# Beside the expert matrix of a two-layer block: five early blocks ahead of the picks, and a main part that begins with a parked unit

## The chip, the cores and the metric

One core of a Trainium2 chip runs the whole computation in one launch. The metric is the device time in microseconds, the median of several runs. Beside the runs there is one profiled execution, whose trace is read below. Its engines are named PE (TensorE, matmuls), PEld (TensorE's weight loads), DVE (VectorE), ACT (ScalarE), POOL (GpSimd) and SP (SyncE, which only issues transfers here).

## What is computed

256 tokens of width 1024 pass through a first transformer block and then a second one. What matters here is the last layer of the second, a product-key mixture of experts with 16384 experts, in float32:

```python
def peer(h, w_q, sub_keys, u, v):            # h: 256 tokens x 1024
    ...
        q = (xb @ w_q).reshape(tb, PEER_HEADS, 2, PEER_DKEY // 2)
        s = jnp.einsum('thpd,hpnd->thpn', q, sub_keys).astype(jnp.float32)
        sv, si = lax.top_k(s, k)                       # 16 best of 128, per head and half
        ...
        top_v, top_i = lax.top_k(cand, k)              # 16 best pairs per head
        experts = jnp.take_along_axis(cand_idx, top_i, axis=-1)
        g = jax.nn.softmax(top_v, axis=-1)
        u_e = u[experts]
        v_e = v[experts]
        a = jax.nn.gelu(jnp.einsum('td,thkd->thk', xb, u_e).astype(jnp.float32), approximate=False)
        return jnp.einsum('thk,thkd->td', (g * a).astype(xb.dtype), v_e)
```

After it come the gated residual and a final norm.

## The kernel before

The kernel gathers no rows. It computes GELU(u · h) for all 16384 experts, multiplies it with a matrix G that holds the weight of each expert for each token (zero for nearly all), and multiplies the result with all of v. The experts are cut into 64 units of 256. A unit of u is 1 MB in two blocks of 1024 words a partition; so does a unit of v.

Each block of weights comes by a transfer into one of 5 ring slots. ScalarE rounds it to a high part (line 1051), and VectorE (line 1437) or GpSimd (line 2085) makes the low part by subtraction; `lo_on_pool` says which. TensorE multiplies high with high, high with low and low with high. Every engine has its own program and runs it in order; `hi_until`, `lo_until` and `load_until` do their part for all blocks up to a key and `AHEAD` = 3 more (1 more in the part beside G on ScalarE and VectorE).

The last layer has three stretches.

1. **Selection** (`SELECT_ORDER`). The scores and the top-16 searches run on VectorE, with help of GpSimd. TensorE meanwhile makes the query panels and the first 11 units of u (`feature_panel`, lines 654 and 659: a block is 16 matmuls with the high part of u and 8 with the low part). The GELU of an early unit is stored to HBM ("parked", `early_out`, line 1345).
2. **The expert matrix** (`expert_matrix_order`). The picks, that is rows, columns and weights of the chosen experts, are transposed (line 1008) once VectorE has made the weight (line 1972). Then come 64 steps of G: VectorE and ScalarE build matrices of zeros and ones (lines 1984, 1388, 1987, 1994), TensorE multiplies them (line 1017), ScalarE copies the one half of a bank to G (line 1375), VectorE adds the other (line 2001). Between the steps stand the blocks of 36 more early units, numbers 11 to 46. Block b belongs to unit 11 + b // 2; 11b stands for the second block of unit 11, and so on. The picks come behind two blocks; three blocks stand between picks and the first step of G. ScalarE takes an early unit's GELU four entries of the order later.
3. **The main part** (`UNIT_ORDER`). It goes through all 64 units. The 17 late ones (47 to 63) are made there by `unit_panel` (lines 681 and 686), summed on VectorE (lines 2035, 2036), GELU on ScalarE (line 1404). The 47 parked ones are loaded from HBM to one of three hid buffers. These buffers lie where G's selection matrices lay. Either kind is multiplied by G on VectorE (line 2042), rounded on ScalarE (line 1406), and its left part is made on VectorE (line 1738, which gives `hid_lo`). Then `rows_onto` (lines 716 and 721) multiplies it with the rows of v, two places in the order later (`V_LAG` = 2), onto four banks `peer_acc`. The order before begins 47, 0, 1, 48, 2, 3, 4, 49.

TensorE takes banks with `take`, which gives the longest idle of the eight and waits until its last user has emptied it. In the second stretch three banks serve u (`u_banks`), four serve picks and G (`G_banks`), and one holds constants ("numbers"). At its end the idle ones stand in this order: those of units 44 and 45, the two of G's step 62, the two of step 63, that of unit 46, and the constants'. Before the first panel of the main part, the program takes four for `peer_acc`, then two for unit 47.

SyncE's program loads the parked unit of place `at + 1` behind the blocks of place `at`; each load waits until its buffer is free.

## Time and profile before

| | |
|---|---|
| runs | median 1392.35 us (1391.27 to 1392.82, 3 runs) |
| profiled execution | 1391.79 us |
| its span, first to last instruction | 1390.0 us |
| mean granted clock of TensorE | 0.992 |
| PE busy | 1351.1 us (97%) |
| DVE busy | 1017.1 us (73%) |
| ACT busy | 756.5 us (54%) |
| POOL busy | 460.1 us (33%) |
| HBM read / written | 270.34 MB / 14.94 MB |

Times in the trace are microseconds from the start of the span. In this execution the picks are transposed at about 692 us, G's steps go from 702 to 923 us, and the main part follows. A line of the timeline gives start and duration, engine, source line, what is written and read, and in brackets the idle time of that engine just before and what ended it. Consecutive matmuls are pipelined, so the duration of one line overlaps the next by some tenths; the difference of two starts is the exact pace.

### The profile page before, as it was taken

To read this page: it belongs to the slowest core of one execution; us is meant where nothing else is said; L and a number is where in the kernel's file an instruction comes from. 1 tells how busy PE (TensorE), PEld (TensorE's weight loads), DVE (VectorE), ACT (ScalarE), POOL (GpSimd) and SP (SyncE) were. 2 spreads that over 40 slices of the span, in tenths; PEclk is the share of its full clock that TensorE was granted. 3 is DMA by queue.
4 is the path that set the end of the run, shared out by engine and by line. 5 is a ranking of instruction groups with operands and counts; after the bars stand their busy time and mean duration, and the time that the engine had idled before them with its cause. 6 is when DMAs were issued, how large, how long until landed. Compare 5 with 4: busy or idle time off the path is not lost.

```text
span 1390.0 us, 21698 instructions
## 1 busy us (share of the span) xinstructions
PE 1351.1 (97%) x8475; PEld 1214.4 (87%) x8475; DVE 1017.1 (73%) x1834; ACT 756.5 (54%) x1201; POOL 460.1 (33%) x264
## 2 busy tenths in 40 slices
PE   9999999999999999999799999989999999999997
PEld 7898889999988777999799999987888888888885
DVE  5676686888867675799888888865666666667666
ACT  5555745444656454554477777754444544544543
POOL 2630000000034102798867777641222222222221
PEclk9999999999999999999999999999999999999999
DMA  7553247879878624467566666654757756767665
GB/s 250 179 146 103 78 172 244 277 266 326 274 245 284 242 99 167 137 207 226 175 185 199 200 191 195 207 184 166 232 200 227 235 197 232 234 198 229 231 200 211
DMA packets 194645, 286.69 MB, mean 206 GB/s; under 512 B 9664, under 2 KB 121024, under 8 KB 194288
## 3 DMA queue, kind: packets, MB, share of 16 engines
q1 hardware_dynamic: 186800, 270.12, 60.2%
q10 hardware_dynamic: 7344, 13.95, 2.6%
q0 software_dynamic: 400, 1.25, 0.4%
q8 instruction: 67, 1.10, 0.3%
q14 instruction: 34, 0.28, 0.1%
HBM read 270.34 MB, written 14.94 MB: 205 GB/s over the span
## 4 chain that ended last, share of the span: by engine, by line
PE 81%; DVE 11%; ACT 2%; DMA 2%; POOL 1%; issue 1%; DVEq 0%; ACTq 0%
PE bank L716 19%; PE bank L654 19%; PE bank L721 10%; PE bank L659 9%; PE bank L627 6%; PE bank L681 5%; PE bank L631 3%; PE bank L686 2%; PE bank L1017 2%; DMA sb_raw<-w_in 1%; PE bank L931 1%; PE bank L950 1%; DVE sb_in_row L1930 1%; PE bank L809 1%; DVE sb_eq L1936 1%
## 5 line engine op out<-in xcount | busy, mean ns | idle before, releaser
L2085 POOL TENSOR_TENSOR sb_lo<-sb_raw,sb_hi 128x1024 fp32r<-128x1024 f32 (+1 forms) x162 | 387.7, 2402 | 596.4 <-ACT sb_hi L1051 596.4
L1051 ACT ACTIVATE sb_hi<-sb_raw 128x1024 fp32r<-128x1024 f32 (+2 forms) x428 | 442.3, 1046 | 202.5 <-DMA sb_raw<-w_in 43.0
L1437 DVE TENSOR_TENSOR sb_lo<-sb_raw,sb_hi 128x1024 fp32r<-128x1024 f32 (+2 forms) x266 | 357.0, 1357 | 159.8 <-ACT sb_hi L1051 158.5
L654 PE MATMUL bank<-sb_act,sb_hi 128*128 128x256 f32 x2720 | 357.4, 284 | 0.7 <-DVE sb_act L1523 0.7
L654 PEld LDWEIGHTS bank<-sb_act,sb_hi 128*128 128x128 f32 x2720 | 340.3, 192 | 2.3 <-issue 1.3
L716 PE MATMUL bank<-sb_hi,sb_hid_hi 128*128 128x512 f32 x600 | 234.8, 391 | 4.1 <-DVE sb_hid_lo L1738 4.1
L716 PE MATMUL bank<-sb_hi,sb_hid_lo 128*128 128x512 f32 x600 | 234.5, 391 | 0.0
L659 PE MATMUL bank<-sb_act,sb_lo 128*128 128x256 f32 x1360 | 191.2, 283 | 2.3 <-POOL sb_lo L2085 2.3
L659 PEld LDWEIGHTS bank<-sb_act,sb_lo 128*128 128x128 f32 x1360 | 175.3, 192 | 3.1 <-POOL sb_lo L2085 3.1
L721 PE MATMUL bank<-sb_lo,sb_hid_hi 128*128 128x512 f32 x600 | 161.0, 389 | 0.0
L716 PEld LDWEIGHTS bank<-sb_hi,sb_hid_hi 128*128 128x128 f32 x600 | 113.3, 189 | 27.1 <-DVE sb_hid_lo L1738 4.3
L716 PEld LDWEIGHTS bank<-sb_hi,sb_hid_lo 128*128 128x128 f32 x600 | 113.3, 189 | 22.9
L721 PEld LDWEIGHTS bank<-sb_lo,sb_hid_hi 128*128 128x128 f32 x600 | 112.6, 188 | 23.4
L1406 ACT ACTIVATE sb_hid_hi<-sb_hid 128x512 fp32r<-128x512 f32 x64 | 40.5, 632 | 127.5 <-DVE sb_hid L2042 127.5
L2091 POOL TENSOR_TENSOR sb_stat<-sb_stat 128x1 f32<-128x1 f32 (+1 forms) x19 | 12.6, 673 | 281.8 <-DVE sb_stat L1467 234.1
L1984 DVE TENSOR_TENSOR sb_hot<-bank,sb_pick_T 128x1024 fp32r<-128x1024 f32 x64 | 78.4, 1224 | 31.8 <-PE bank L1017 31.8
L1738 DVE TENSOR_TENSOR sb_hid_lo<-sb_hid,sb_hid_hi 128x512 fp32r<-128x512 f32 x75 | 51.9, 693 | 52.4 <-ACT sb_hid_hi L1406 44.7
L627 PE MATMUL bank<-sb_hi,sb_act 128*128 128x512 f32 (+1 forms) x352 | 83.9, 380 | 1.0 <-DVE sb_act L1523 0.6
L1453 DVE CUSTOM_DVE_ANT_0 sb_ada_junk<-sb_ada_w,sb_c_rows 128x1024 bf16<-128x1024 f32 x64 | 79.4, 1275 | 0.0
L627 PEld LDWEIGHTS bank<-sb_hi,sb_act 128*128 128x128 f32 x352 | 63.2, 188 | 13.1 <-ACT sb_hi L1051 1.9
L681 PE MATMUL bank<-sb_act,sb_hi 128*128 128x512 f32 x272 | 68.6, 395 | 3.2 <-DVE sb_G L2001 3.2
L681 PEld LDWEIGHTS bank<-sb_act,sb_hi 128*128 128x128 f32 x272 | 50.4, 190 | 13.2 <-issue 3.4
(346 smaller groups left out, 1581.5 us busy)
## 6 DMA issues: line engine op xcount, KB each, us to landing
sb_raw<-peer_uT SPq DMA_DIRECT2D x128, 512.0 KB, 4.0
sb_raw<-peer_v SPq DMA_DIRECT2D x128, 512.0 KB, 4.5
sb_raw<-w_in SPq DMA_DIRECT2D x52, 512.0 KB, 4.5
sb_ada_w<-ada_wT SPq DMA_DIRECT2D x48, 512.0 KB, 6.0
parked_units<-sb_early ACTq DMA_DIRECT2D x47, 256.0 KB, 4.1
sb_hid<-parked_units SPq DMA_DIRECT2D x47, 256.0 KB, 2.7
sb_raw<-w_gate SPq DMA_DIRECT2D x22, 512.0 KB, 4.0
sb_raw<-w_up SPq DMA_DIRECT2D x22, 512.0 KB, 5.1
```

The source lines that it names most:

```text
L627: e.matmul(opened[t][:, 0:n], part[:, k0 + k, t * P:(t + 1) * P], hi[:, k, :], start=i == first_i and k == 0 and part is x.hi, stop=False)
L654: e.matmul(bank[:, j * T:(j + 1) * T], hi[:, k, j * P:(j + 1) * P], part[:, k0 + k, :], start=i == first_i and j == 0 and k == 0 and part ...
L659: ins = e.matmul(bank[:, j * T:(j + 1) * T], lo[:, k, j * P:(j + 1) * P], x.hi[:, k0 + k, :], start=False, stop=i == last_i and j == 1 and ...
L681: e.matmul(bank[j][:, :].rearrange("p (w t) -> p w t", w=2), hi[:, k, j * P:(j + 1) * P], act_both[:, k0 + k], start=first and k == 0, sto ...
L716: e.matmul(psum(acc, 2 * half_ + t)[:, :], part[:, k, t * P:(t + 1) * P], hi[:, k, :], start=first and k == 0 and part is hid.hi, stop=False)
L721: ins = e.matmul(psum(acc, 2 * half_ + t)[:, :], hid.hi[:, k, t * P:(t + 1) * P], lo[:, k, :], start=False, stop=last and k == 1)
L1051: e.activation(flat_of(i, "hi"), flat_of(i, "raw"), ACT.Copy).then_inc(hi_done[i % R], 1)
L1437: e.tensor_tensor(flat_of(i, "lo"), flat_of(i, "raw"), flat_of(i, "hi").bitcast(F32), ALU.subtract).then_inc(lo_done[i % R], 1)
L1453: e.tensor_tensor_reduce(ada_junk[n % 2], ada_bufs[b], c_rows[:, row], 1.0, 0.0, ALU.mult, ALU.add, mcol[name][:, c:c + 1]).then_inc(*ada_ ...
L1738: e.tensor_tensor(hid_pair[i].lo, hid_raw[i], hid_pair[i].hi.bitcast(F32), ALU.subtract).then_inc(*hid_lo.inc(*unit))
L1984: e.tensor_tensor(h[:, :, 0:3:2, :].rearrange("p t w n -> p w t n"), iota_p.unsqueeze(1).unsqueeze(1).to_broadcast([P, 2, TG, P]), pT[:, 0 ...
L2085: e.tensor_tensor(flat_of(i, "lo"), flat_of(i, "raw"), flat_of(i, "hi").bitcast(F32), ALU.subtract).then_inc(lo_done[i % R], 1)
```

## The change

- `expert_matrix_order`: the picks come behind five blocks of u, and the first step of G behind nine (`b + 1 - G_FROM` is first positive at b = 8), so four blocks stand between them. 38 early units stand there instead of 36, so 49 units are parked and 15 are late.
- `UNIT_ORDER`: the main part begins with parked unit 0, and goes on 49, 1, 2, 3, 50, 4, 5, 6, 51. Three times four parked units stand in a row, where before there were at most three.
- TensorE takes the banks of `peer_acc` only with v's first rows, behind the first late unit's panel.
- ScalarE and VectorE make the high and low parts of the first late unit's blocks between G's last two sums.
- SyncE loads the first parked unit ahead of the main loop, once G's step 62 is full.

```diff
-EARLY_BESIDE_G = 36
+EARLY_BESIDE_G = 38
...
-G_FROM = 4
+PICKS_FROM, G_FROM = 5, 8
...
-UNIT_ORDER = [v for k in range(N_LATE) for v in (EARLY + k, *range(k * EARLY // N_LATE, (k + 1) * EARLY // N_LATE))]
+UNIT_ORDER = [0] + [v for k in range(N_LATE) for v in (EARLY + k, *range(1 + k * (EARLY - 1) // N_LATE, 1 + (k + 1) * (EARLY - 1) // N_LATE))]
...
-        if b == G_FROM // 2 - 1:
+        if b == PICKS_FROM - 1:
             yield "picks", 0, 0
...
-            for b in range(4):
-                take("peer_acc", b)
             for at in range(N_UNITS + V_LAG):
                 if at < N_UNITS and UNIT_ORDER[at] >= EARLY:
                     whole(unit_panel(UNIT_ORDER[at], h2))
                 if at >= V_LAG:
                     v = at - V_LAG
+                    if v == 0:
+                        for b in range(4):
+                            take("peer_acc", b)
                     rows_onto("peer_acc", ("v", v), ("peer", v), v == 0, v == N_UNITS - 1)
...
-            for q in range(N_G - HOT_BUFS, N_G):
-                G_rounded(q)
+            G_rounded(N_G - 2)
+            hi_until(("uT", UNIT_ORDER[1]), None, 0)
+            G_rounded(N_G - 1)
...
-            for q in range(N_G - HOT_BUFS, N_G):
-                G_sum(q)
+            G_sum(N_G - 2)
+            lo_until(("uT", UNIT_ORDER[1]), None, 0)
+            G_sum(N_G - 1)
...
+            def load_hid(at):
+                i, u = at % HID_BUFS, UNIT_ORDER[at]
+
+                sp.wait_ge(*(hid_used["peer", at - HID_BUFS] if at >= HID_BUFS else full("G", N_G - (1 if at else 2), TG - TG_BANK)))
+                b, nth = early_slot(u)
+                sp.wait_ge(early_stored[b], 16 * (nth + 1))
+                e.dma_start(hid_raw[i], parked_units[u].rearrange("p (c t) -> p c t", t=T)).then_inc(hid_in[i], 16)
+
+            load_hid(0)
             for at in range(N_UNITS + V_LAG):
...
                 if at + 1 < N_UNITS and UNIT_ORDER[at + 1] < EARLY:
-                    i, u = (at + 1) % HID_BUFS, UNIT_ORDER[at + 1]
-                    sp.wait_ge(*(hid_used["peer", at + 1 - HID_BUFS] if at + 1 >= HID_BUFS else full("G", N_G - 1, TG - TG_BANK)))
-                    b, nth = early_slot(u)
-                    sp.wait_ge(early_stored[b], 16 * (nth + 1))
-                    e.dma_start(hid_raw[i], parked_units[u].rearrange("p (c t) -> p c t", t=T)).then_inc(hid_in[i], 16)
+                    load_hid(at + 1)
```

## Rows read from the trace of the kernel before

**Rows 1.** The page's DMA issues: KB each, median us from issue to landing.
```profile
sb_hid<-parked_units SPq DMA_DIRECT2D x47, 256.0 KB, 2.7
```

**Rows 2.** TensorE's waits: releaser, us in total, times, longest.
```profile
PE bank L1008 <- DVE sb_weight L1972: 6.9, 1, 6.9
```

**Rows 3.** Timeline of TensorE around the picks.
```profile
678.73 2.08 PE L654 MATMUL bank<-sb_act,sb_hi 128*128 128x256 f32 x16
...
681.61 2.08 PE L654 MATMUL bank<-sb_act,sb_hi 128*128 128x256 f32 x16
...
691.59 0.66 PE L1008 MATMUL bank<-sb_const,sb_pick 128*128 128x128 f32 x2 [6.94 <-DVE sb_weight L1972]
...
692.75 3.10 PE L654 MATMUL bank<-sb_act,sb_hi 128*128 128x256 f32 x16
...
702.40 0.64 PE L1017 MATMUL bank<-sb_hot 128*128 128x256 f32 x4
```

**Rows 4.** Timeline of VectorE in the selection.
```profile
641.52 0.33 DVE L1930 SCALAR_TENSOR_TENSOR sb_in_row<-sb_abf,sb_topi 128x32 f32<-128x32 f32 x1
...
643.55 1.22 DVE L1437 TENSOR_TENSOR sb_lo<-sb_raw,sb_hi 128x1024 fp32r<-128x1024 f32 x1
...
677.19 2.32 DVE L1930 SCALAR_TENSOR_TENSOR sb_in_row<-sb_abf,sb_topi 128x32 f32<-128x32 f32 x1
...
689.20 2.24 DVE L1972 TENSOR_TENSOR sb_weight<-sb_topv,sb_stat 128x256 f32<-128x256 f32 x1
```

**Rows 5.** Timeline of ScalarE ahead of the picks.
```profile
684.94 0.42 ACT L1360 ACTIVATE sb_topv<-sb_topv 128x256 f32<-128x256 f32 x1 [6.59 <-DVE sb_topv L1965]
...
687.67 2.95 ACT L1051 ACTIVATE sb_hi<-sb_raw 128x1024 fp32r<-128x1024 f32 x3 [0.40 <-ACT sb_early L1345]
```

**Rows 6.** Timeline of GpSimd: ahead of the picks, and in the main part.
```profile
688.80 7.20 POOL L2085 TENSOR_TENSOR sb_lo<-sb_raw,sb_hi 128x1024 fp32r<-128x1024 f32 x3 [4.62 <-ACT sb_hi L1051]
...
945.21 2.39 POOL L2085 TENSOR_TENSOR sb_lo<-sb_raw,sb_hi 128x1024 fp32r<-128x1024 f32 x1 [13.22 <-ACT sb_hi L1051]
```

**Rows 7.** Timeline of TensorE at the start of the main part.
```profile
925.12 1.12 PE L659 MATMUL bank<-sb_act,sb_lo 128*128 128x256 f32 x8
929.48 2.94 PE L681 MATMUL bank<-sb_act,sb_hi 128*128 128x512 f32 x8 [3.24 <-DVE sb_G L2001]
...
940.98 0.80 PE L716 MATMUL bank<-sb_hi,sb_hid_hi 128*128 128x512 f32 x1 [4.12 <-DVE sb_hid_lo L1738]
...
948.01 1.98 PE L681 MATMUL bank<-sb_act,sb_hi 128*128 128x512 f32 x8
...
953.57 0.40 PE L716 MATMUL bank<-sb_hi,sb_hid_hi 128*128 128x512 f32 x1
...
959.04 0.39 PE L716 MATMUL bank<-sb_hi,sb_hid_hi 128*128 128x512 f32 x1
```

**Rows 8.** Timeline of VectorE at the start of the main part.
```profile
927.75 1.47 DVE L2001 TENSOR_TENSOR sb_G<-bank,sb_G 128x256 f32<-128x256 f32 x4 [6.90 <-ACT sb_G L1375]
...
936.42 0.42 DVE L2035 COPY sb_hid<-bank 128x256 f32<-128x256 f32 x1 [1.08 <-PE bank L686]
...
938.84 0.69 DVE L2042 TENSOR_TENSOR sb_hid<-sb_hid,sb_G 128x512 f32<-128x512 f32 x1 [0.76 <-ACT sb_hid L1404]
940.23 0.69 DVE L1738 TENSOR_TENSOR sb_hid_lo<-sb_hid,sb_hid_hi 128x512 fp32r<-128x512 f32 x1 [0.70 <-ACT sb_hid_hi L1406]
...
946.11 2.57 DVE L1437 TENSOR_TENSOR sb_lo<-sb_raw,sb_hi 128x1024 fp32r<-128x1024 f32 x1 [1.21 <-ACT sb_hi L1051]
```

**Rows 9.** Timeline of ScalarE at the start of the main part.
```profile
926.34 0.60 ACT L1345 ACTIVATE sb_early<-bank 128x512 f32<-128x512 f32 x1 [6.12 <-PE bank L659]
...
927.34 1.25 ACT L1375 ACTIVATE sb_G<-bank 128x256 f32<-128x256 f32 x4 [0.40 <-ACT sb_early L1345]
928.43 3.92 ACT L1051 ACTIVATE sb_hi<-sb_raw 128x1024 fp32r<-128x1024 f32 x4
```

**Rows 10.** Busy us by engine in a 2 us stretch, then granted clock, DMA share, GB/s.
```profile
932.00:934.00 2.00, 2.00 (x10) 1.91 (x10) 2.00 (x2) 0.35 (x1) 0.00 (x0) 0.54 0.02 6
```

## The prediction

> **What bounds the kernel now.** I read the list of TensorE's waits first. TensorE is the bound almost everywhere, so only the places where it stands still, or runs at the lower clock, can be sold. The longest wait is in [rows 2], 6.9 us for the picks. The next two stand in brackets in [rows 7]: 4.12 us for the left part of a hidden unit and 3.24 us for a sum of G. Together that is 14.3 us, and all three are places that the diff touches.
>
> Then TensorE's timeline around the picks [rows 3]. The second block in front of the picks starts at 681.61; a block lasts 2.88 us (678.73 to 681.61), so it ends at 684.5. The transposes of the picks start at 691.59, and three blocks later G's first product starts at 702.40. From 684.5 to 702.40 are 17.9 us, for 8.64 us of blocks and the transposes. The remainder is more than the 6.94 us of idle time: the first 16 matmuls after it take 3.10 us against 2.08, because the clock is still low. The reader is to see that a stall costs twice, once as idle time and once as slow matmuls behind it.
>
> Last, the start of the main part [rows 7]. The last early block ends at 926.1. TensorE idles 3.24 us, runs the panel of unit 47, idles 4.12 us, and starts v's first rows at 940.98. In the second of these stretches the granted clock is 0.54 [rows 10], mostly the lower level, 1.2 GHz. From 929.48 the panel takes until 936.86 (940.98 less 4.12), 7.38 us, where the next one takes 5.56 (948.01 to 953.57): 1.8 us lost. v's first unit takes 7.03 us (940.98 to 948.01), the second 5.47 (953.57 to 959.04): 1.56 us lost.
>
> **The picks.** Nothing of the selection moves on VectorE: it ends with the weight at 689.20 plus 2.24, 691.4 [rows 4]. What moves is TensorE's work: blocks 12a, 12b and 13a now stand in front of the transposes. Their operands set the pace.
> - 12a follows at 684.5. Its rounding (ScalarE) was made before ScalarE began to wait for the exponential, since ScalarE rounds three blocks ahead there. It ends at 687.4.
> - 12b's rounding is queued on ScalarE behind the exponential (684.94), which waits for VectorE. It is the first of three that start at 687.67 and take 2.95 us together [rows 5]. So it is there at 688.7, and TensorE waits 1.3 us. Its low part is GpSimd's, the first of three from 688.80, 7.20 us together [rows 6], there at 691.2. TensorE is through its first 16 matmuls at 690.6, waits 0.6 us, and ends 12b at 692.2.
> - 13a has both operands (689.7 and 693.6) when they are needed and ends at 695.0. The picks have been ready since 691.4. The transposes took 1.16 us at the low clock (691.59 to 692.75); at the higher level I take 0.7.
>
> So the same three blocks and the transposes are done at 695.8 instead of 702.40: 6.6 us gained. Bounds: 7.3 if 12b does not wait at all, 5.5 if the short waits drop the clock for one block (the 1.02 us seen behind the long stall).
>
> G's own chain then starts about 3.3 us later than before against the same instants, but relative to TensorE it now has four blocks (11.5 us) until its first product instead of three. G's first product at 702.40 had no wait ahead of it [rows 3], so there was room and there is more now. The blocks that stand beside G's 64 steps are as many as before, 68 (72 less 4, 76 less 8): no gain or loss there.
>
> **Two more units beside G.** Each is two early blocks, 5.76 us; each saves a panel of 5.56 us in the main part [rows 3, 7]. Twice 0.20 is 0.4 us more work. VectorE is spared their copies and sums, which costs and gains nothing, as it does not bind there. Two more parked units are stored and loaded (256 KB, 2.7 us to landing [rows 1]), beside matmuls.
>
> **The start of the main part.** I write this in the instants of before, with 926.1 as the end of the last early block.
> - Unit 49's panel takes the two oldest banks, those of units 46 and 47. Unit 47's bank was emptied long ago, so TensorE does not wait for G: 3.24 us of idle time go, and so does the slow panel behind it.
> - Panel 49, first block: until 928.9. ScalarE first does GELU of the last early unit at 926.34, then two of G's four copies (927.34 and 1.25 us for four, so 0.63), then the rounding of 49b (0.98, from 3.92 for four [rows 9]), ready at 929.0. Its low part is GpSimd's, 2.40 us, 931.45. TensorE waits 0.1 and 0.6 us and ends the panel at 932.4.
> - G's last copies end at 929.6, its last sums (1.47 us for four [rows 8]) near 930.2. Then VectorE multiplies parked unit 0, whose load was released 6 us before 926.1 and has landed. But GpSimd is in its subtraction until 931.45. VectorE's own subtraction with two operands in SBUF took 2.57 us at 946.11 [rows 8] while GpSimd's ran from 945.21 [rows 6]: it finished 1.08 us after GpSimd's did. So I let the multiply begin at 931.45. From the multiply to the left part took 2.08 us (938.84 to 940.92 [rows 8]): 933.5.
> - v's first rows also need a rounding, and ScalarE makes it only after the parked unit's own: 931.45 + 1.39 + 0.98 = 933.9. TensorE starts v's first unit there, after 1.5 us of waiting, and is through at 939.3. Its four banks, G's, were given back by 930.2.
> - Unit 49 is next, and here a wait comes back. VectorE has first three low parts to make (933.85 on, 1.22 us each [rows 4], until 937.5), then copies to left part, 4.50 us (936.42 to 940.92): 942.0. TensorE waits 2.7 us.
>
> At 942.0 instead of 940.98 the kernel stands 1.0 us later, but has one v unit (5.47 us) behind it: 4.4 us gained. The slow matmuls behind the wait I charge as before, 1.56 us, since a wait of 2.7 is nearest to the 3.24 that was followed by the low clock [rows 7, 10]; the bound on the other side is no loss, 1.6 us more gained.
>
> The Trainium skill, SBUF — State Buffer, the section on the two sides of SBUF, says that GpSimd and a VectorE operation with two SBUF inputs exclude each other for a whole instruction. By it the multiply waits as above, and a wait could also fall on GpSimd; if they could overlap, the sum would be 1.2 us better. The rows at 945.21 and 946.11 agree with it.
>
> **The sum.** 6.6 − 0.4 + 4.4 = 10.6 us. The profiled execution took 1391.79 us (span 1390.0), so it becomes 1381.2; the median of the runs stands 0.56 above the profiled one: 1381.8 us. Differences below 0.2% (2.8 us) hardly show.
>
> **Rivals.**
> - *More is gained* (0.15). No clock loss behind the 2.7 us wait (1.6) and the multiply not held by GpSimd (1.2): 13.4 us, 1379.0. For it: the wait is shorter than both that were followed by the low clock. Against it: my own schedule has another wait of 1.5 us, 8 us ahead of it.
> - *The main part gains nothing* (0.12). The wait moves behind unit 49 entirely: v's first unit is done at 939.3, and unit 49's left part would have to come 4.4 us later than 942.0, for example if its low parts wait for blocks of v that the synchronizing queue loads late, behind the parked unit's load. That load waits for G's last step but one, some 6 us before 926.1, so I see no lateness. Time 1386.2.
> - *The picks gain nothing* (0.07). The blocks in front starve, and only 4.0 us remain: 1388.4. It needs 12b and 13a to come as late as the picks did.
> - *Slower* (0.02). GpSimd's subtractions for the further blocks fall beside the selection and hold VectorE's small operations: one of 0.33 us took 2.32 at 677.19, beside GpSimd [rows 4], 2.0 us each. Five more operations held would eat the 10.6 us; from seven on, the time is above 1395. Against it: 12b's subtraction cannot start before its rounding at 688.7, and then only the weight is left on VectorE, which is already held (2.24 us).
> - *Nothing changes* (0.02): all waits return elsewhere, 1392.
>
> The forecast itself has 0.62. Faster by over 0.2% in all cases but the last two: 0.96; same 0.02; slower 0.02. The range reaches from the better rival with its bounds, 1378.8, to the rival without the main part's gain, 1386.0.
>
> **What the new profile would show.** In front of the picks five blocks, with a wait of about 1.3 us for ScalarE's rounding and about 0.6 us for GpSimd in the fourth, and none of VectorE's weight. No wait of TensorE for G's sum. A wait of about 1.5 us ahead of v's first rows, and one of 2 to 3 us for the left part of unit 49, with a low clock behind it. The prediction is wrong if the weight ends later than 7 us after the second block, if unit 49's panel waits for a bank, or if TensorE waits in the runs of four parked units in a row, which before had at most three: there v and a parked unit ask for 1.25 MB in 5.47 us.

## The result, and the profile after

The changed kernel takes 1379.71 us (median of 4 runs, 1378.80 to 1381.42), the kernel before 1392.16 us beside it (4 runs, 1391.27 to 1392.82). The ratio is 0.9911, its 95% interval 0.9900 to 0.9922: 12.4 us faster, by the interval 10.9 to 13.9. The forecast was 1381.8 us. The profiled execution of the changed kernel took 1381.42 us with a span of 1379.6, 10.4 us shorter than the span before, so this pair of profiles shows 2 us less gain than the medians do. That difference has a place, told below.

TensorE's waits after the change, longest of those that the diff touches (releaser, us in total, times, longest):

```profile
PE bank L716 <- DVE sb_hid_lo L1740: 2.2, 1, 2.2
...
PE bank L654 <- ACT sb_hi L1052: 1.2, 1, 1.2
PE bank L716 <- ACT sb_hi L1052: 1.0, 1, 1.0
```

The wait for the weight [rows 2] and the wait for G's sum [rows 7] are gone from the list; instead of 14.3 us in three waits there are 4.4 in three, and two more of 0.3 us each, both for GpSimd's low parts.

TensorE's timeline around the picks, which answers to [rows 3]:

```profile
681.95 2.08 PE L654 MATMUL bank<-sb_act,sb_hi 128*128 128x256 f32 x16
...
684.83 2.08 PE L654 MATMUL bank<-sb_act,sb_hi 128*128 128x256 f32 x16
...
689.10 2.18 PE L654 MATMUL bank<-sb_act,sb_hi 128*128 128x256 f32 x16 [1.24 <-ACT sb_hi L1052]
691.58 1.22 PE L659 MATMUL bank<-sb_act,sb_lo 128*128 128x256 f32 x8 [0.30 <-POOL sb_lo L2088]
692.64 2.08 PE L654 MATMUL bank<-sb_act,sb_hi 128*128 128x256 f32 x16
...
695.53 0.38 PE L1008 MATMUL bank<-sb_const,sb_pick 128*128 128x128 f32 x2
...
696.10 2.15 PE L654 MATMUL bank<-sb_act,sb_hi 128*128 128x256 f32 x16
```

11b starts at 681.95, 0.34 us later than the same block before (681.61). Its follower starts without a wait; 12b waits 1.24 us for ScalarE's rounding and 0.30 for GpSimd's subtraction; the transposes follow with no wait. Five blocks and the transposes are done at 696.1; before, that point was G's first product at 702.40, 702.74 when the 0.34 is added. The difference is 6.6 us. The first block behind the transposes takes 2.15 us: the clock stayed up.

TensorE's timeline at the start of the main part, which answers to [rows 7]. The last early block ends at 931.37, where the first line of L681 starts:

```profile
931.37 2.00 PE L681 MATMUL bank<-sb_act,sb_hi 128*128 128x512 f32 x8
933.21 1.11 PE L686 MATMUL bank<-sb_act,sb_lo 128*128 128x256 f32 x8
934.32 2.14 PE L681 MATMUL bank<-sb_act,sb_hi 128*128 128x512 f32 x8
936.80 1.21 PE L686 MATMUL bank<-sb_act,sb_lo 128*128 128x256 f32 x8 [0.35 <-POOL sb_lo L2088]
939.05 0.47 PE L716 MATMUL bank<-sb_hi,sb_hid_hi 128*128 128x512 f32 x1 [1.03 <-ACT sb_hi L1052]
...
946.91 0.50 PE L716 MATMUL bank<-sb_hi,sb_hid_hi 128*128 128x512 f32 x1 [2.18 <-DVE sb_hid_lo L1740]
```

The panel begins at once. v's first unit starts 7.68 us after the last early block (939.05 less 931.37). Unit 49's rows of v start 15.54 us after it, behind a wait of 2.18 us; the prediction had 15.9 and 2.7. What it had not is the next row. The stretch behind this wait, busy us by engine, then the granted clock, DMA share and GB/s:

```profile
946.00:948.00 2.00, 1.09 (x5) 0.92 (x6) 1.29 (x2) 0.64 (x2) 0.00 (x0) 1.00 0.94 313
```

The granted clock is 1.00, the upper of the two levels, 2.4 GHz, where [rows 10] has 0.54 behind the wait of 3.24 us. The unit behind the wait takes 5.72 us (946.91 to 952.63), against 5.44 for two undisturbed blocks of 2.72: a loss of 0.28 us where 1.56 was charged.

VectorE's timeline there, which answers to [rows 8]:

```profile
934.57 0.86 DVE L2003 TENSOR_TENSOR sb_G<-bank,sb_G 128x256 f32<-128x256 f32 x2 [0.64 <-ACT sb_G L1376]
...
935.54 1.75 DVE L2045 TENSOR_TENSOR sb_hid<-sb_hid,sb_G 128x512 f32<-128x512 f32 x1
937.99 0.69 DVE L1740 TENSOR_TENSOR sb_hid_lo<-sb_hid,sb_hid_hi 128x512 fp32r<-128x512 f32 x1 [0.70 <-ACT sb_hid_hi L1408]
938.93 3.50 DVE L1439 TENSOR_TENSOR sb_lo<-sb_raw,sb_hi 128x1024 fp32r<-128x1024 f32 x3 [0.25 <-ACT sb_hi L1052]
942.35 0.42 DVE L2038 COPY sb_hid<-bank 128x256 f32<-128x256 f32 x1
```

The multiply of the parked unit takes 1.75 us instead of 0.69. GpSimd's subtraction, the only operation on that engine there, ends at 936.74:

```profile
934.34 2.40 POOL L2088 TENSOR_TENSOR sb_lo<-sb_raw,sb_hi 128x1024 fp32r<-128x1024 f32 x1 [10.33 <-ACT sb_hi L1052]
```

So the hold of 1.06 us that the prediction counted is there. Then come the three low parts in a row, as foreseen, which keep the copies of unit 49's banks waiting until 942.35.

Behind that the main part has no wait of TensorE at all, the three runs of four parked units included.

**The end.** At the end stands something on which the prediction says nothing. VectorE's first operation of the gated residual, before (first fence) and after (second fence), in the timelines of VectorE:

```profile
1377.63 0.70 DVE L2055 TENSOR_TENSOR bank<-bank,sb_slot 128x512 f32<-128x512 f32 x1 [4.07 <-DMA sb_slot<-parked_g]
```

```profile
1367.26 0.70 DVE L2058 TENSOR_TENSOR bank<-bank,sb_slot 128x512 f32<-128x512 f32 x1 [5.48 <-DMA sb_slot<-parked_g]
```

It multiplies with a gate row that was parked in HBM. The load, 512 KB, goes through the ring behind v's last rows. The chain of work that ended last shows it in the changed kernel:

```profile
1360.18 7.05 DMA sb_slot<-parked_g
```

It took 7.05 us there and some 5.5 before (issued 1372.15). TensorE's last group (the last line of L721) starts at 1379.66 before and at 1367.70 after, 11.96 us earlier. From there to the end of the span are 10.3 us before and 11.9 after. So 1.6 us of the 12.0 were given back in the profiled execution, by one late load. In the profiles of two more executions of the same changed kernel (after_again and after_third, below) this load took 5.49 and 4.83 us, and the stretch 10.4 and 9.7 us; there TensorE's last group starts at 1367.95 and 1368.90, 11.7 and 10.8 us earlier than before. That fits medians that do not carry the loss, but the runs behind the medians have no traces of their own.

### The profile page after: what moved, and what is told of

It reads as the page before. It is cut to its first block, busy times and chain, and to the rows that moved or that the text cites. A ratio compares the mean times of both kernels' runs of the same rounds, so it can differ in the third digit from the quotient of the medians.

```text
span 1379.6 us, 21759 instructions
## 1 busy us (share of the span) xinstructions
PE 1347.5 (98%) x8507; PEld 1212.3 (88%) x8507; DVE 1011.4 (73%) x1823; ACT 753.9 (55%) x1201; POOL 468.1 (34%) x267
## 4 chain that ended last, share of the span: by engine, by line
PE 80%; DVE 12%; ACT 3%; DMA 2%; POOL 1%; issue 1%; DVEq 0%; ACTq 0%
PE bank L716 19%; PE bank L654 19%; PE bank L659 10%; PE bank L721 10%; PE bank L627 6%; PE bank L681 4%; PE bank L631 3%; PE bank L1017 2%; PE bank L686 2%; DVE sb_lo L1439 1%; ACT sb_hi L1052 1%; PE bank L931 1%; PE bank L950 1%; POOL sb_lo L2088 1%; DVE sb_in_row L1932 1%
## 5 line engine op out<-in xcount | busy, mean ns | idle before, releaser
L2088 POOL TENSOR_TENSOR sb_lo<-sb_raw,sb_hi 128x1024 fp32r<-128x1024 f32 (+1 forms) x165 | 394.9, 2404 | 575.6 <-ACT sb_hi L1052 575.6
L1439 DVE TENSOR_TENSOR sb_lo<-sb_raw,sb_hi 128x1024 fp32r<-128x1024 f32 (+2 forms) x263 | 353.0, 1359 | 151.8 <-ACT sb_hi L1052 150.0
L654 PE MATMUL bank<-sb_act,sb_hi 128*128 128x256 f32 x2784 | 364.6, 284 | 2.2 <-ACT sb_hi L1052 1.2
L654 PEld LDWEIGHTS bank<-sb_act,sb_hi 128*128 128x128 f32 x2784 | 346.9, 192 | 3.9 <-ACT sb_hi L1052 1.4
L659 PE MATMUL bank<-sb_act,sb_lo 128*128 128x256 f32 x1392 | 195.9, 283 | 2.7 <-POOL sb_lo L2088 2.7
L659 PEld LDWEIGHTS bank<-sb_act,sb_lo 128*128 128x128 f32 x1392 | 179.5, 192 | 3.7 <-POOL sb_lo L2088 3.7
L721 PE MATMUL bank<-sb_lo,sb_hid_hi 128*128 128x512 f32 x600 | 161.1, 389 | 0.0
L721 PEld LDWEIGHTS bank<-sb_lo,sb_hid_hi 128*128 128x128 f32 x600 | 112.6, 188 | 23.6 <-POOL sb_lo L2088 0.3
L681 PE MATMUL bank<-sb_act,sb_hi 128*128 128x512 f32 x240 | 59.8, 391 | 0.0
L2003 DVE TENSOR_TENSOR sb_G<-bank,sb_G 128x256 f32<-128x256 f32 x128 | 51.5, 449 | 8.5 <-ACT sb_G L1376 8.4
```

Source lines behind the costliest of these rows:

```text
L654: e.matmul(bank[:, j * T:(j + 1) * T], hi[:, k, j * P:(j + 1) * P], part[:, k0 + k, :], start=i == first_i and j == 0 and k == 0 and part ...
L659: ins = e.matmul(bank[:, j * T:(j + 1) * T], lo[:, k, j * P:(j + 1) * P], x.hi[:, k0 + k, :], start=False, stop=i == last_i and j == 1 and ...
L681: e.matmul(bank[j][:, :].rearrange("p (w t) -> p w t", w=2), hi[:, k, j * P:(j + 1) * P], act_both[:, k0 + k], start=first and k == 0, sto ...
L721: ins = e.matmul(psum(acc, 2 * half_ + t)[:, :], hid.hi[:, k, t * P:(t + 1) * P], lo[:, k, :], start=False, stop=last and k == 1)
L1439: e.tensor_tensor(flat_of(i, "lo"), flat_of(i, "raw"), flat_of(i, "hi").bitcast(F32), ALU.subtract).then_inc(lo_done[i % R], 1)
L2088: e.tensor_tensor(flat_of(i, "lo"), flat_of(i, "raw"), flat_of(i, "hi").bitcast(F32), ALU.subtract).then_inc(lo_done[i % R], 1)
```

## The experiments

Twelve kernels ran, two of them the changed kernel again, in three groups of four, each group on one chip (the first and the third on the same one) with nine runs of the kernel before: medians 1391.41, 1391.59 and 1390.92. A ratio is always to those. The first group has no run of the changed kernel, so its four kernels can be set against it only by way of these ratios. All but two have five runs, the last two have four. A diff is against the changed kernel.

### The two parts alone

picks_alone keeps the five blocks ahead of the picks and the 38 units, and puts the rest back:

```diff
-UNIT_ORDER = [0] + [v for k in range(N_LATE) for v in (EARLY + k, *range(1 + k * (EARLY - 1) // N_LATE, 1 + (k + 1) * (EARLY - 1) // N_LATE))]
+UNIT_ORDER = [v for k in range(N_LATE) for v in (EARLY + k, *range(k * EARLY // N_LATE, (k + 1) * EARLY // N_LATE))]
...
+            for b in range(4):
+                take("peer_acc", b)
             for at in range(N_UNITS + V_LAG):
...
-            G_rounded(N_G - 2)
-            hi_until(("uT", UNIT_ORDER[1]), None, 0)
-            G_rounded(N_G - 1)
+            for q in range(N_G - HOT_BUFS, N_G):
+                G_rounded(q)
...
-            load_hid(0)
```

> One part alone: picks behind five blocks and 38 units beside G; the main part begins as before with a late unit, its banks taken first, G's last sums together. If the two parts are independent, this gives what the trace of the changed kernel shows around the picks, 6.6 us less 0.4 us for two more early units: 6.2 us below the kernel before, near 1386.0. In the trace TensorE waits 1.2 us for ScalarE's rounding and 0.3 us for GpSimd in front of the picks, and as before about 3.2 us for the sum of G and 4.1 us for the left part, with the low clock behind each. Rival: the gain at the picks is only lent and comes back as a wait of G's first steps, which now start later against VectorE: then 1392 and a wait at G's products.

Measured: 1386.78 us (1385.05 to 1387.41), ratio 0.9958 (0.9944 to 0.9971), 4.6 us faster. The expectation was 6.2 us. There is no wait for the weight, and the waits at the main part's start are back. TensorE's timeline:

```profile
934.04 3.52 PE L681 MATMUL bank<-sb_act,sb_hi 128*128 128x512 f32 x8 [3.25 <-DVE sb_G L2001]
...
945.43 0.80 PE L716 MATMUL bank<-sb_hi,sb_hid_hi 128*128 128x512 f32 x1 [4.12 <-DVE sb_hid_lo L1738]
```

start_alone leaves the picks where they were:

```diff
-EARLY_BESIDE_G = 38
+EARLY_BESIDE_G = 36
...
-PICKS_FROM, G_FROM = 5, 8
+PICKS_FROM, G_FROM = 2, 4
```

> The other part alone: picks behind two blocks and 36 units beside G as before, but the main part begins with a parked unit. From the changed kernel's trace: v's first unit earlier by 5.4 us, the left part of the late unit 0.6 us later, and 1.3 us less of low clock, so 6.1 us below the kernel before, near 1386.1, if TensorE again waits 2.2 us and keeps the high clock. Rival, as my prediction charged it: the wait of 2 to 3 us is followed by the low clock, and only 4.4 us are gained, 1387.8.

Measured: 1386.55 us (1384.15 to 1387.40), ratio 0.9958 (0.9944 to 0.9972), 4.9 us faster. Here the wait for the weight is 6.9 us again, and the waits for the left part (2.1) and for ScalarE (1.0) are those of the changed kernel. TensorE's path did what was expected: the clock stays at 1.00 behind the wait for the left part, and from the last early block (925.97) to TensorE's last group (1373.48) it takes 447.5 us, 6.05 less than before (453.56). The medians show 4.9 of it.

What follows: each part gains without the other, and by medians about half. The two sum to 9.5 us, 1.7 to 2.9 short of what both gave together in three groups of runs (12.4, 11.7, 11.2). Part of this is to be seen in the profile of picks_alone. From the last early block to TensorE's last group it takes 444.2 us, where before it is 442.4 once the two panels of 5.56 that became early units are taken off. The windows show why: behind the wait of 4.12 us the clock stays down longer. Before (first fence), and picks_alone (second):

```profile
942.00:944.00 2.00, 2.00 (x6) 1.61 (x5) 1.29 (x2) 0.64 (x2) 0.00 (x0) 0.50 0.00 0
944.00:946.00 2.00, 2.00 (x10) 1.58 (x10) 0.69 (x1) 2.00 (x3) 0.79 (x1) 0.98 0.00 0
```

```profile
944.00:950.00 6.00, 4.57 (x11) 3.62 (x12) 3.28 (x5) 3.26 (x5) 0.35 (x1) 0.50 0.07 23
```

In picks_alone v's first two units take 13.53 us (945.43 to the next panel at 958.96), 2.65 more than four blocks of 2.72; before, 1.56 were lost. So behind the same wait of 4.12 us one profile lost 1.1 us more than the other. About another microsecond is what start_alone's median gained less than its TensorE path did (4.9 against 6.05). That, and what may be left of the gap, I can't place; a microsecond is within the scatter of the medians.

### The banks, and the interleaved sums

banks_first takes v's four banks ahead of the panel again:

```diff
+            for b in range(4):
+                take("peer_acc", b)
             for at in range(N_UNITS + V_LAG):
...
-                    if v == 0:
-                        for b in range(4):
-                            take("peer_acc", b)
```

> The changed kernel with one part undone: the four banks of v's sums are taken ahead of the first late unit's panel, as before. The panel then gets G's last banks and waits for G's last sum, about 4.0 us (from 931.4 to 935.3 in the changed kernel's trace), with 1.5 us of slow matmuls behind it. If the banks' order is what removed the wait, the panel ends about 5 us later, and as 3.2 us of waiting behind it (1.0 ahead of v, 2.2 ahead of the late unit's rows) take up a part, the kernel is slower than the changed one by 2 to 4 us: near 1382.7. Rival: the later wait takes up all of it, less than 1 us.

Measured: 1381.41 us (1380.11 to 1381.73), ratio 0.9923 (0.9910 to 0.9937). Its TensorE timeline:

```profile
935.04 3.66 PE L681 MATMUL bank<-sb_act,sb_hi 128*128 128x512 f32 x8 [4.09 <-DVE sb_G L2002]
...
942.28 0.40 PE L716 MATMUL bank<-sb_hi,sb_hid_hi 128*128 128x512 f32 x1
```

The panel now waits 4.09 us for G's sum, and its first matmuls take 3.66 us instead of 2.00. Yet v's first unit then starts with no wait, and unit 49's rows at 947.75 with none either. Only 0.7 to 1.1 us is lost on TensorE's path (the stretch from the last early block to TensorE's last group, 437.4 against 436.3 to 436.8 in the three profiles of the changed kernel), less than the 2 to 4 that I expected. The medians gain 10.0 us where the changed kernel gains 11.2 to 12.4; the intervals overlap. The stall of 4.09 replaces the later three. The wait of 0.35 was for GpSimd; the other two hang on the same VectorE program, the sums, the multiply, the low parts, the left part, which runs here at nearly the same distances as in the changed kernel (unit 49's copies begin 11.2 us after the last early block, there 11.0). The late taking of the banks is worth about 1 us by itself. The rest belongs to the order that begins with a parked unit, together with its early load and the interleaved sums; no kernel has that order alone.

sums_together makes G's last two copies and sums in one go, ahead of the first late unit's operands:

```diff
-            G_rounded(N_G - 2)
-            hi_until(("uT", UNIT_ORDER[1]), None, 0)
-            G_rounded(N_G - 1)
+            for q in range(N_G - HOT_BUFS, N_G):
+                G_rounded(q)
...
-            G_sum(N_G - 2)
-            lo_until(("uT", UNIT_ORDER[1]), None, 0)
-            G_sum(N_G - 1)
+            for q in range(N_G - HOT_BUFS, N_G):
+                G_sum(q)
```

> The changed kernel with another part undone: ScalarE makes G's last two copies together and then the rounding of the late unit's second block. Theory: the rounding comes 0.7 us later, so TensorE waits longer in the panel (about 1 us), but G is complete earlier, and the multiply of the parked unit begins before GpSimd's subtraction and is not held by it; v's first unit and the late unit's rows then start 0.5 to 0.9 us earlier, and the kernel is equal to 0.7 us faster than the changed one. Rival, what the order in the change would be good for: the late rounding delays everything behind it by 0.7 us, slower by that.

Measured: 1381.62 us (1380.88 to 1383.76), ratio 0.9931 (0.9917 to 0.9944). In its VectorE timeline the multiply runs unheld, since GpSimd's operand is not there yet:

```profile
935.06 0.69 DVE L2043 TENSOR_TENSOR sb_hid<-sb_hid,sb_G 128x512 f32<-128x512 f32 x1
```

and TensorE waits in the panel instead:

```profile
937.41 2.11 PE L681 MATMUL bank<-sb_act,sb_hi 128*128 128x512 f32 x8 [2.72 <-ACT sb_hi L1052]
```

I had misread ScalarE's order. 49b's rounding then stands behind the rounding of the parked unit itself, which waits for the multiply. Unit 49's rows of v start 15.94 us after the last early block instead of 15.54. I had expected this kernel to be equal or up to 0.7 us faster; it came out on the other side, as the rival had it. The next panel starts 27.13 us after the last early block, in the changed kernel 26.73: the interleaving gains 0.4 us on this path. Over the whole stretch to TensorE's last group even that is not to be seen (436.7 against 436.3 to 436.8), and the medians, 9.8 us gained against 11.2 to 12.4, can't be told apart with certainty. The wait of 2.72 us is as long as the one that the prediction charged with slow matmuls, and none follow it. The stretch behind it, in the same columns as above, the granted clock being 1.00:

```profile
938.00:940.00 2.00, 1.62 (x8) 1.03 (x6) 1.66 (x1) 2.00 (x3) 1.84 (x1) 1.00 0.07 25
```

### Where the rest of the main part's start goes

after_again and after_third are the changed kernel once more, one in each of the other two groups.

> The changed kernel once more, as the base for the kernels beside it: 1379.7 us, 12.4 below the kernel before. If the prediction had been right in every term but the clock, the gain would be 12.2 with no low clock behind the 2.2 us wait. In the last stretch the load of the parked gate row ends up to 3 us after the first bank of v's sums is full; it took 7.0 us in the changed kernel's profile and 5.5 in that of before, so the runs may spread by 1 to 3 us with it.

> The changed kernel as the base on this chip: 1379.8 us, 11.8 to 12.4 below the kernel before.

Measured: 1379.85 us (1379.28 to 1380.71), ratio 0.9912 (0.9899 to 0.9926), and 1379.71 us (1378.81 to 1380.91), ratio 0.9918 (0.9904 to 0.9931). Both have the waits of the first profile; the wait for the left part is 2.1 and 2.2 us, again at the full clock.

two_parked begins the main part with two parked units, and has ScalarE round v's first blocks sooner:

```diff
-UNIT_ORDER = [0] + [v for k in range(N_LATE) for v in (EARLY + k, *range(1 + k * (EARLY - 1) // N_LATE, 1 + (k + 1) * (EARLY - 1) // N_LATE))]
+UNIT_ORDER = [0, 1] + [v for k in range(N_LATE) for v in (EARLY + k, *range(2 + k * (EARLY - 2) // N_LATE, 2 + (k + 1) * (EARLY - 2) // N_LATE))]
...
-            hi_until(("uT", UNIT_ORDER[1]), None, 0)
+            hi_until(("uT", UNIT_ORDER[2]), None, 0)
             G_rounded(N_G - 1)
+            hi_until(("uT", UNIT_ORDER[2]), None, 2)
...
-                        hi_until(("uT", u))
+                        hi_until(("uT", u), None, AHEAD + (at == 2))
```

> The main part begins with two parked units (0, 1, 49, 2, 3, 50), ScalarE rounds v's first two blocks behind G's last copy, and one block more ahead of the late unit's GELU. Theory: the 2.2 us wait of TensorE for the left part of unit 49 is a matter of order, since VectorE's chain from the copies to the left part has one v unit more to hide behind; both waits in front of v's rows go (1.0 and 2.2 us), with 0.3 us of slow matmuls: about 3 us faster than the changed kernel, 1376.8. Rival: the chain on VectorE and ScalarE is simply longer by the second parked unit (2.1 us), and the wait moves to the next block of v: less than 1 us.

Measured: 1379.76 us (1378.24 to 1383.03), ratio 0.9914 (0.9897 to 0.9931). The expectation was 3 us faster than the changed kernel; its median is that of after_again, as the rival had it. In place of the waits of 1.03 and 2.14 us stand 0.92, 0.87 and 0.39; the waits of this stretch sum to 2.6 instead of 3.5. One thing that stands in the way of more is that VectorE and GpSimd now subtract at the same time. VectorE's and GpSimd's timelines:

```profile
940.76 5.69 DVE L1440 TENSOR_TENSOR sb_lo<-sb_raw,sb_hi 128x1024 fp32r<-128x1024 f32 x3
```

```profile
942.09 3.28 POOL L2089 TENSOR_TENSOR sb_lo<-sb_raw,sb_hi 128x1024 fp32r<-128x1024 f32 x1 [5.17 <-ACT sb_hi L1052]
```

Three low parts take 5.69 us instead of 3.50, and GpSimd's one 3.28 instead of 2.40: each holds the other. In the profiles the stretch from the last early block to TensorE's last group is still 1.2 us shorter than in after_again (435.6 against 436.8), and 0.5 of that goes at the late load of the gate row (the end takes 10.9 us against 10.4).

vector_order keeps the order of units and changes VectorE's: unit 49's copies come between the first and the second of the three low parts, and the third only behind unit 49's left part.

```diff
-                        lo_until(("uT", u))
+                        lo_until(("uT", u), None, 1 if at == 1 else AHEAD)
...
+                        if at == 1:
+                            lo_until(("uT", u), None, 2)
                         dve.wait_ge(*unit_gelu.at(u))
...
                     hid_left(("peer", at), i)
+                    if at == 1:
+                        lo_until(("uT", u))
```

> The changed kernel with VectorE's order at the first late unit altered: one low part of v, then the copies and sums of unit 49, the second low part while ScalarE makes the GELU, the third behind the unit's left part. Theory: the wait of TensorE for unit 49's left part (2.1 to 2.2 us) is set by VectorE's queue, three low parts of 3.5 us together ahead of the copies; with two of them behind, the left part comes 1.8 us earlier and the wait falls to about 0.4 us: 1.8 us faster than the changed kernel, 1378.0. Rival: the wait is set by ScalarE or by when unit 49's panel ends, and it stays at 2 us.

Measured: 1379.47 us (1378.37 to 1381.33), ratio 0.9919 (0.9905 to 0.9932). TensorE's timeline:

```profile
944.35 0.50 PE L716 MATMUL bank<-sb_hi,sb_hid_hi 128*128 128x512 f32 x1 [0.16 <-DVE sb_hid_lo L1740]
...
947.70 0.50 PE L716 MATMUL bank<-sb_hi,sb_hid_hi 128*128 128x512 f32 x1 [0.29 <-ACT sb_hi L1052]
...
950.17 1.20 PE L721 MATMUL bank<-sb_lo,sb_hid_hi 128*128 128x512 f32 x4 [0.36 <-POOL sb_lo L2092]
```

The cause of the 2.18 us wait is thereby shown. With two low parts taken from in front of unit 49's left part it shrinks to 0.16, and v's rows of unit 49 start 13.56 us after the last early block instead of 15.54. But of these 2.0 us only 0.85 last, where 1.8 were expected: the next panel starts 25.88 us after the last early block, in after_third 26.73. v's second block of unit 49, with its operands made later, now waits 0.29 and 0.36 us. The wait had been hiding these. The median, 0.2 us below after_third, can't be told from it.

### The end

g2_early loads the gate row in the middle of the main part, to where the picks' transposes lay, and not through the ring:

```diff
-    plain(("end_g2",), parked_g2, 1, D)
...
+        g2late, g2late_in = place("g2late", D, F32, OFF["pick_T"]), sem("g2late_in")
...
-                    own(e.tensor_tensor(bank, bank, g2[:, 0, c], ALU.mult))
+                    own(e.tensor_tensor(bank, bank, g2late[:, c], ALU.mult))
...
+                if at == N_UNITS // 2:
+                    sp.wait_ge(*full("G", N_G - 1, TG - TG_BANK))
+                    sp.wait_ge(early_stored[3], 16 * EARLY_BESIDE_G)
+                    e.dma_start(g2late, parked_g2).then_inc(g2late_in, 16)
```

> The changed kernel with the parked gate row loaded in the middle of the main part, to words that G's picks and the fourth early buffer held, and no ring slot for it. In the changed kernel's profile the first bank of v's sums is full at 1364.5 and VectorE starts at 1367.3, when the row has landed. Theory: the end waits for this load, so 1.5 to 2.8 us are gained (1.5 is what the profile of before would give), unless the load of the parked x, issued 2.7 us ahead of it, lands no earlier. Rival: the end is set by that load or by the last bank, and at most 0.5 us is gained.

Measured: 1381.08 us (1378.74 to 1381.89), ratio 0.9919 (0.9905 to 0.9934). The profile does what was asked. VectorE's timeline:

```profile
1364.52 0.70 DVE L2058 TENSOR_TENSOR bank<-bank,sb_g2late 128x512 f32<-128x512 f32 x1 [3.07 <-PE bank L721]
```

VectorE now waits for TensorE's first bank alone and starts when that is full. The end, from TensorE's last group, takes 9.05 us, against 10.35 in after_again. The profiled span is the shortest of its group (1376.9 us), but the median is 1.2 us above after_again. By itself it is inconclusive: its five runs spread over 3.2 us.

two_parked_g2 and vector_order_g2 join it to the two kernels above.

> Two parked units first, and the gate row loaded early. From the profiles of the two kernels: 1.0 us less waiting at the start of the main part and 1.3 us less behind the last matmul: 2.3 us faster than the changed kernel, 1377.5. Rival, as the runs of each alone had it: no difference that can be told, 1379.8.

> VectorE's altered order and the early gate row together. If both theories hold, 1.8 and 1.3 us: 3.1 us faster than the changed kernel, 1376.7. Rival: 1379.8, as neither wait was worth its length.

Measured: 1378.21 us (1377.44 to 1379.57, 4 runs), ratio 0.9910 (0.9895 to 0.9926), and 1377.83 us (1377.35 to 1378.52, 4 runs), ratio 0.9906 (0.9890 to 0.9921). The expectations were 1377.5 and 1376.7. In both the end takes 9.0 to 9.1 us. In the same group all four runs of vector_order_g2 lie below all five of after_third (from 1378.81 up). It has the lowest median here, 1.9 us below the changed kernel, and 13.1 us below the kernel before; two_parked_g2 can't be told from it. Against vector_order alone the early load gives 1.6 us by medians. The profiles agree: the end takes 10.9 us in vector_order, with a load of 5.95 us, and 9.7 in after_third, with one of 4.83, so what VectorE's order gained at the start was lost at the late load in that execution.

### The slower rival

round_ahead lets ScalarE round two more blocks before it waits for the exponential, which should take away the 1.24 us wait of 12b:

```diff
-                    hi_until(("uT", n_e))
+                    hi_until(("uT", n_e), None, AHEAD + (2 if n_e == EARLY_BESIDE_SELECT - 1 else 0))
```

> The changed kernel with ScalarE rounding two blocks more (12b and 13a) before it waits for the exponential. The 1.2 us wait of TensorE in front of 12b would go. But GpSimd then subtracts from 684.5 on without a break, beside the end of the selection on VectorE. Theory: each small operation of VectorE with two operands in SBUF is then held until the end of a subtraction (2.4 us), so the weight ends 2 to 5 us later than 691.8, still not far behind the blocks in front of the picks, which end near 694; the result is between 1.2 us faster and 3 us slower than the changed kernel. Rival: the two engines do not disturb each other, the weight ends as before, and the kernel is 1.5 us faster.

Measured: 1383.15 us (1381.65 to 1383.61), ratio 0.9932 (0.9918 to 0.9945), 3.3 us slower than after_again. With its operands there, GpSimd subtracts earlier, beside the end of the selection. VectorE's timeline of round_ahead:

```profile
683.90 2.30 DVE L1966 COPY sb_stat<-sb_topv 128x16 f32<-128x16 f32 x1
686.24 2.57 DVE L1967 TENSOR_TENSOR sb_topv<-sb_topv,sb_stat 128x256 f32<-128x256 f32 x1
```

and the same two operations in the changed kernel:

```profile
684.59 0.18 DVE L1966 COPY sb_stat<-sb_topv 128x16 f32<-128x16 f32 x1
684.80 0.42 DVE L1967 TENSOR_TENSOR sb_topv<-sb_topv,sb_stat 128x256 f32<-128x256 f32 x1
```

Each is held for 2.1 us. The weight ends at 695.34 instead of 691.81, 3.5 us later (2 to 5 were expected), and TensorE's timeline pays:

```profile
695.48 0.41 PE L1008 MATMUL bank<-sb_const,sb_pick 128*128 128x128 f32 x2 [2.56 <-DVE sb_weight L1974]
...
696.21 3.56 PE L654 MATMUL bank<-sb_act,sb_hi 128*128 128x256 f32 x16
```

It waits 2.56 us at the transposes, and the block behind runs at half the clock (3.56 us against 2.08). From 11b to the end of the last early block round_ahead takes 2.2 us more than after_again (681.25 to 932.88 against 681.73 to 931.17). That is not all of the difference: behind the wait of 2.14 us for unit 49's left part, which both kernels have, its profile shows the low clock, and from there to the next panel it takes 12.62 us against 11.19, 1.4 us that have nothing to do with the held operations. So the mechanism of the "slower" rival is real, at the price of 2 us per held operation that the prediction gave it. It is also far from making the change a loss: with two operations held the kernel is still 8.4 us faster than the one before. What keeps it out of the changed kernel is ScalarE's own wait for the exponential, which delays 12b's rounding and with it GpSimd. The 1.24 us wait that looks like a fault is cheaper than the 2.2 us.

The Trainium skill, SBUF — State Buffer, "SBUF: two separate sides", calls the pair of ports that VectorE and GpSimd share an exclusive lock, held for a whole instruction by whichever starts first. The trace agrees: 1.75 us instead of 0.69 for the multiply, 2.57 instead of 0.42 here. The Trainium skill, SBUF — State Buffer, "Who interferes with whom", counts a plain copy among the operations that can take the shared pair; the copy of 16 columns that took 2.30 us instead of 0.18 agrees with that too.

## Why the prediction was right, point by point

The median came 2.1 us below the forecast, inside the range. TensorE's path accounts for 1.4 of it (12.0 against 10.6) and the lower median of the kernel before for 0.2; the rest is not placed. The terms, read as differences on TensorE's path from the two profiles:

| term | predicted | measured |
|---|---|---|
| picks | +6.6 | +6.6 |
| two more units beside G | −0.4 | −0.4 |
| start of the main part | +4.4 | +6.1 |
| work ahead of the picks | 0 | −0.3 (11b starts at 681.95, not 681.61) |
| TensorE's last group | +10.6 | +12.0 (1379.66 to 1367.70) |
| the end | 0 | −1.6 in this execution |

The measured +6.1 is what is left of the stretch from the last early block to TensorE's last group: 453.56 us before, 11.12 off for two panels, is 442.44; after 436.33. The −0.4 stands here as predicted, four blocks of 2.88 against two panels of 5.56; the rows of the picks and the panels in the changed kernel have the same pace. The +6.1 is of the first profile: in after_again and after_third the stretch is 436.8 us, which makes it +5.7, and in start_alone it is +6.05. Of the −0.3 most is already there at 561 us (a block of the selection starts at 561.05, before at 560.78), behind a wait of 2.33 us at 554 which is followed by the low clock in both profiles, for longer after the change.

- **The picks.** Right step by step. 12b waits for ScalarE, 1.24 us against 1.3, and for GpSimd, 0.30 against 0.6; the picks were ready when TensorE reached them. The bound of 5.5, with a clock that drops behind the short waits, did not come true: the blocks behind them take 2.08 and 2.15 us. The bound of 7.3 on the other side was summed too low: without the two waits of 12b, 1.9 us, the prediction's own instants give 8.5, with the picks ready all the same at 691.4. round_ahead takes these two waits away, and there the picks come 3.5 us later.
- **The banks.** TensorE does not wait for G's sum, and the panel runs at full pace. That part alone is worth only about 1 us, as banks_first shows, because VectorE's program is what the stretch ends on either way. The prediction didn't separate this.
- **v's first unit.** At 7.68 us after the last early block, predicted 7.8 (933.9 less 926.1). GpSimd's hold on the multiply was there (1.06 us, predicted 1.2), and sums_together shows the multiply without it at 0.69 us.
- **The wait that comes back.** There, in its place, for the reason given, 2.18 us against 2.7. vector_order shows the reason.
- **The clock behind it: this term was mis-sized.** "The slow matmuls behind the wait I charge as before, 1.56 us". Measured: 0.28 us; in all three profiles of the changed kernel the granted clock behind this wait is 1.00. I took the wait of 2.7 as nearest to the 3.24 that was followed by the low clock, and that row says nothing of a shorter wait; sums_together has one of 2.72 us with the clock at 1.00 behind it, round_ahead one of 2.14 with the low clock. This, 1.3 us, and 0.36 us on the instant of 946.91 make up the 1.7 us between 4.4 and 6.1. The better rival's first condition came true, its second (no hold by GpSimd) didn't.
- **The end.** The prediction let the gain pass through to the end in full. In the profiled execution the gate row's load took it back by 1.6 us. With loads of 5.49 and 4.83 us in the two other profiles the end cost nothing against before. The medians differ by 12.4 us, about as much as TensorE's path gained (12.0), which fits a loss of that execution alone. g2_early removes the dependence.
- **The other rivals.** "The main part gains nothing" and "the picks gain nothing" are refuted by start_alone and picks_alone. "Slower" is refuted too: its mechanism shows in round_ahead, one parameter away, but two held operations leave the kernel 8.4 us faster than before.

What stays open: why a wait of 2.1 to 2.7 us is followed by the low clock in some executions and not in others, and the last microsecond between medians that should be equal.

## What to carry to other kernels

Moving ready work in front of a stall can pay twice, for the idle time and for the slow matmuls behind it, but only as far as the operands of the moved work come through engines that aren't themselves waiting: follow each in-order program, not only the stalled one. Before an operand is made earlier on one engine, look whose ports that occupies; here a 1.24 us wait was shielding the selection from losing 3.5 us. And when the bound is shortened by microseconds, look at the last loads of the kernel: they are issued by the same ring and can keep part of the gain.

## What the hardware showed unexpectedly

- Whether the clock falls behind a wait of 2.1 to 2.7 us is not settled by its length. Behind 2.18 us (946.91) the granted clock is 1.00, and behind 2.72 us in sums_together (937.41) too. Behind a wait of 2.14 us at 948.4 in round_ahead it is 0.57 from 948 to 952, and its wait of 2.56 us at the transposes was followed by 0.50. All waits of 3.24 us and more were. An earlier wait of 2.3 us, at 554 us in every kernel here, is followed by the low clock in 7 of the 14 profiles and goes either way in the same kernel. The windows of the changed kernel, its first profile and after_again:

```profile
554.00:556.00 2.00, 1.90 (x9) 1.93 (x10) 0.35 (x1) 1.12 (x3) 0.00 (x0) 0.52 0.00 0
```

```profile
554.00:556.00 2.00, 1.65 (x15) 1.68 (x16) 0.60 (x2) 1.57 (x4) 0.00 (x0) 1.00 0.00 0
```

  The price there is small: from this wait's end to the block near 561 us are 6.95 us in the first and 6.49 in the second, because at the full clock TensorE then waits 1.08 us for VectorE.

- The same load of 512 KB took 7.05, 5.49 and 4.83 us from issue to landing in three executions of the same kernel, at the one place where nothing covers it.
- A copy of 128 x 16 words within SBUF took 2.30 us beside GpSimd's subtractions and 0.18 without them; the operation behind it, 16 times as large, lost as much (2.57 against 0.42).
